# RWKV inverses on packed 32x32 diagonal blocks instead of 64x64 blocks

## The reference: one step of a hybrid trunk

```python
def step(S, inp):                       # per token
    r_t, w_t, k_t, v_t, kk_t, a_t = inp
    sa = jnp.einsum('bhvk,bhk->bhv', S, -kk_t)
    S = (S * w_t[:, :, None, :] + sa[..., None] * (kk_t * a_t)[:, :, None, :]
         + v_t[..., None] * k_t[:, :, None, :])
    return S, jnp.einsum('bhvk,bhk->bhv', S, r_t)
```

## Time and profile before

| | us |
|---|---|
| Median of 3 runs | 1288.97 (1288.81 to 1289.48) |
| The profiled execution: its time | 1288.66 |
| Its span (first to last instruction) | 1286.8 |
| PE busy | 1229.0 (96%) |
| DVE busy | 920.9 (72%) |
| ACT busy | 716.3 (56%) |
| The stage with the inverses, layer 0 | 72 to 165 |
| The same stage, layer 1 | 590 to 685 |

### The profile page before, as it was taken

How to read it: one execution, slowest core, us unless ns; L and a number is a source line. 1 busy time by engine, 2 the same in 40 slices (tenths; PEclk the granted TensorE clock), 3 DMA queues, 4 the chain that set the end, 5 groups by cost and what they waited for, 6 DMA issues and landing times.

```text
span 1286.8 us, 27073 instructions
## 1 busy us (share of the span) xinstructions
PE 1229.0 (96%) x10557; PEld 1098.7 (85%) x10557; DVE 920.9 (72%) x1477; ACT 716.3 (56%) x1109; POOL 131.5 (10%) x161
## 2 busy tenths in 40 slices
PE   7989999899999999998999989899999999999996
PEld 6979888789999999997988878887888788788785
DVE  7576755666555557857675565588989989998996
ACT  6633345234433334472434534577877878777784
POOL 1021310210000000102121012001010110101010
PEclk9999999789999999999999988999999999999998
DMA  8321331155445443242133106389979979997992
GB/s 295 120 85 46 111 106 35 73 198 188 150 152 168 152 147 132 75 134 70 54 119 107 35 23 232 122 292 330 341 256 356 323 263 344 324 354 253 358 323 104
DMA packets 63835, 236.35 MB, mean 184 GB/s; under 512 B 7536, under 2 KB 7760, under 8 KB 63088
## 3 DMA queue, kind: packets, MB, share of 16 engines
q1 hardware_dynamic: 60960, 221.51, 49.1%
q0 software_dynamic: 2336, 12.81, 2.7%
q10 hardware_dynamic: 432, 0.52, 0.1%
HBM read 225.41 MB, written 8.09 MB: 181 GB/s over the span
## 4 chain that ended last, share of the span: by engine, by line
PE 82%; DVE 10%; ACT 4%; issue 4%; DMA 0%; DVEq 0%; ACTq 0%
PE bank L619 12%; PE bank L621 11%; PE bank L620 11%; PE bank L1409 8%; PE bank L1386 6%; PE bank L1388 6%; PE bank L1387 6%; PE bank L613 3%; PE bank L1306 2%; DVE wlo L1981 2%; ACT whi L1472 2%; PE bank L813 1%; PE bank L802 1%; PE bank L809 1%; PE bank L1351 1%
## 5 line engine op out<-in xcount | busy, mean ns | idle before, releaser
L1472 ACT ACTIVATE whi<-wraw 128x1024 fp32r<-128x1024 f32 x407 | 428.8, 1059 | 354.7 <-PE bank L621 292.5
L1981 DVE TENSOR_TENSOR wlo<-wraw,whi 128x1024 fp32r<-128x1024 f32 x407 | 501.4, 1245 | 170.4 <-ACT whi L1472 162.9
L619 PE MATMUL bank<-hh,whi 128*128 128x320 f32 x576 | 189.1, 328 | 12.6 <-DVE Dx L2095 6.4
L621 PE MATMUL bank<-hh,wlo 128*128 128x320 f32 x576 | 180.5, 313 | 0.0
L620 PE MATMUL bank<-hl,whi 128*128 128x320 f32 x576 | 180.5, 313 | 0.0
L1386 PE MATMUL bank<-whi,hh 128*128 128x512 f32 (+1 forms) x384 | 147.4, 384 | 3.4 <-DVE wlo L1981 2.9
L1388 PE MATMUL bank<-wlo,hh 128*128 128x512 f32 (+1 forms) x384 | 143.5, 374 | 0.0
L1387 PE MATMUL bank<-whi,hl 128*128 128x512 f32 (+1 forms) x384 | 143.3, 373 | 0.0
L619 PEld LDWEIGHTS bank<-hh,whi 128*128 128x128 f32 x576 | 110.3, 191 | 23.9 <-issue 7.9
L619 PE MATMUL bank<-rawh,whi 128*128 128x320 f32 x384 | 119.8, 312 | 0.5 <-DVE rawl L2538 0.3
L621 PE MATMUL bank<-rawh,wlo 128*128 128x320 f32 x384 | 118.9, 310 | 0.0
(11 more groups left out here) (427 smaller groups left out, 2084.4 us busy)
## 6 DMA issues: line engine op xcount, KB each, us to landing
wraw<-in_w SPq DMA_DIRECT2D x410, 512.0 KB, 5.0
smb<-in_s_ssm POOLq DMA_DIRECT2D x2, 1536.0 KB, 8.0
out_o_ssm<-smb POOLq DMA_DIRECT2D x2, 1536.0 KB, 7.2
cst<-in_consts SPq DMA_DIRECT2D x1, 2097.0 KB, 13.3
srw<-in_s_rwkv POOLq DMA_DIRECT2D x2, 768.0 KB, 5.9
out_o_rwkv<-srw POOLq DMA_DIRECT2D x2, 768.0 KB, 3.7
x<-in_x SPq DMA_DIRECT2D x2, 640.0 KB, 4.9
cBs<-cB SPq DMA_DIRECT2D x16, 80.0 KB, 2.1
```

What stands on the lines that cost most here:

```text
L619: mm(out, hi, rh, start=first, stop=False)
L621: return mm(out, lo, rh, start=False, stop=last)
L1472: af(whi[:, ring % HI, :], wraw[:, POS[ring], :], ACT.Copy).then_inc(S("slot_hi"), 1)
L1981: tt(wlo[:, POS[ring], :], wraw[:, POS[ring], :], whi[:, ring % HI, :].bitcast(F32), ALU.subtract).then_inc(S("slot_split"), 1)
```

## The change

The inverses of the 32x32 diagonal blocks are held by themselves. A matrix of 64x64 on 64 rows becomes two of 32x32: rows 0 to 31 hold the upper left block, rows 32 to 63 the lower right one (u = 0 and 1), and `Wm`, `TM` and a new `Tq` have 32 columns a place. Levels 1 to 4 run on these. `quads` are the four tiles `o32(o, u)` of 32 rows and 32 columns on the array's diagonal. Level 5 of blocks 0 and 1 becomes two products of the 32x32 blocks around the off-diagonal block of A, which DVE has kept unmasked in columns 32 to 63 of `A`, and the full `TT` is then put together. Block 2 has three levels and stays in `Tq`; L881 reads `Tq` on four tiles there. The number of pieces of each part is as before (12, 12 and 6 on PE; 14, 14 and 8 on DVE), and no TURNS list changes. The constants in HBM are smaller by 96 columns.

```diff
 # PE, inverse(l, b)
-                        for r in map(o64, range(2)):
-                            m = mm(B[A_BANK[b]][r, (c * TA + t) * CH:(c * TA + t + 1) * CH], aa[r, t, cs], X2[r, t, cs],
+                        for u in range(2):
+                            us = slice(cs.start + 32 * u, cs.start + 32 * u + 32)
+                            to = cs if b < 2 and u == 0 else us
+                            at, w = (c * TA + t) * CH, to.stop - to.start
+                            for o in range(2):
+                                m = mm(B[A_BANK[b]][o32(o, u), at:at + w], aa[o64(o), t, us], X2[o64(o), t, to],
...
-                    for r in map(o64, range(2)):
-                        m = mm(B[bk][r, h * CH:(h + 1) * CH], Wm[r, b, h, :], C("i64", rows=r), start=True, stop=True)
+                    for r in quads:
+                        m = mm(B[bk][r, h * 32:(h + 1) * 32], Wm[r, b, h, :], C("i32", rows=r), start=True, stop=True)
-                for q in range(1, LEVELS[b]):
+                for q in range(1, min(LEVELS[b], 5)):
...                   # L802, L809, L813 likewise: for r in quads, 32 and 16 columns
+                if LEVELS[b] == 6:
+                    yield
+                    pe.wait_ge(S(f"inv_dve{b}"), inv_dve(l, b, 11))
+                    for h in heads:
+                        for o in range(2):
+                            m = mm(B[bk][o32(o, 1), h * 32:(h + 1) * 32], A[o32(o, 0), b, h, 32:64], TM[o32(o, 0), b, h, :],
+                    m.then_inc(S(f"inv_pe{b}"), 1)
+                    yield
+                    pe.wait_ge(S(f"inv_dve{b}"), inv_dve(l, b, 12))
+                    for h in heads:
+                        at = n * 32 + h * 32
+                        for u in range(2):
+                            for o in range(2):
+                                lo = o32(o, 1)
+                                m = mm(B[bk][o32(o, u), at:at + 32], C("i32", rows=lo) if u else Wm[lo, b, h, :], Tq[lo, b, h, :],
 # PE, rwkv(l, b): L881
-                        for r in map(o64, range(2)):
-                            m = mm(B[SA_BANK[b]][r, t * HD:(t + 1) * HD], TT[r, b, c * TA + t, :], Rs[r, t, :],
+                        for r in [o32(o, u) for u in range(2) for o in range(2)] if b == 2 else map(o64, range(2)):
+                            m = mm(B[SA_BANK[b]][r, t * HD:(t + 1) * HD], Tq[r, b, t, :] if b == 2 else TT[r, b, c * TA + t, :],
 # DVE, inverse(l, b)
+                if b < 2:
+                    for r in (o32(0, 0), o32(1, 0)):
+                        cp(A[r, b, 0:n, 32:64], b64(A_BANK[b], n, r)[:, :, 32:64])
...                   # all masks, sums and levels on 32 columns a place instead of 64
+                if LEVELS[b] == 6:
+                    yield
+                    v.wait_ge(S(f"inv_pe{b}"), inv_pe(l, b, 11))
+                    cp(Wm_, b32(bk, 0, n)).then_inc(S(f"inv_dve{b}"), 1)
+                    yield
+                    v.wait_ge(S(f"inv_dve{b}"), inv_dve(l, b, 11))
+                    tt(TT[:, b, :, 0:32], Tq_, rep(C("low"), n), ALU.mult)
+                    v.wait_ge(S(f"inv_pe{b}"), inv_pe(l, b, 12))
+                    cp(TT[:, b, :, 32:64], b32(bk, n * 32, n)).then_inc(S(f"inv_dve{b}"), 1)
```

More of the change, by code:

```diff
@@ L429, in trunk @@
         top[0] = raw_at + KEEP * D * 4
-        A, Wm, TM = (sb(n, [P, 3, HA, CH]) for n in ("A", "Wm", "TM"))
+        A = sb("A", [P, 3, HA, CH])
+        Wm, TM = (sb(n, [P, 3, HA, 32]) for n in ("Wm", "TM"))
         brx = sb("brx", [P, TA, T])
@@ L501, in half1, with b32, o32 @@
             return ap.rearrange("p (a o s) -> p a o s", o=2, s=1 << q)[:, :, odd, :]
+        def b32(b, lo, k, rows=slice(0, P)):
+            return B[b][rows, lo:lo + k * 32].rearrange("p (a c) -> p a c", c=32)
+        def o32(o, u):
+            return slice(64 * o + 32 * u, 64 * o + 32 * u + 32)
         def o64(o):
@@ L777, in inverse @@
                 c0, nch, bk = BLOCKS[b][0], CHUNKS_OF[b], INV_BANK[b]
-                heads = range(nch * TA)
+                n = nch * TA
+                heads = range(n)
+                quads = [o32(o, u) for u in range(2) for o in range(2)]
                 yield
@@ L800, in inverse @@
                     for h in heads:
-                        for r in map(o64, range(2)):
-                            m = mm(B[bk][r, h * CH:(h + 1) * CH], A[r, b, h, :], TM[r, b, h, :], start=True, stop=True)
+                        for r in quads:
+                            m = mm(B[bk][r, h * 32:(h + 1) * 32], A[r, b, h, 0:32], TM[r, b, h, :], start=True, stop=True)
                     m.then_inc(S(f"inv_pe{b}"), 1)
@@ L879, in rwkv @@
                     for t in range(TA):
-                        for r in map(o64, range(2)):
-                            m = mm(B[SA_BANK[b]][r, t * HD:(t + 1) * HD], TT[r, b, c * TA + t, :], Rs[r, t, :],
-                                   start=True, stop=True)
+                        for r in [o32(o, u) for u in range(2) for o in range(2)] if b == 2 else map(o64, range(2)):
+                            m = mm(B[SA_BANK[b]][r, t * HD:(t + 1) * HD], Tq[r, b, t, :] if b == 2 else TT[r, b, c * TA + t, :],
+                                   Rs[r, t, :], start=True, stop=True)
                     m.then_inc(S("rw_SA"), 1)
@@ L2233, in inverse @@
                     v.wait_ge(S(f"inv_dve{b}"), inv_dve(l, b, 2 * q + 1))
[L2234 removed]
+                    for mt, odd in ((TM_, 0), (Tq_, 1)):
                         if odd or q < LEVELS[b] - 1:
[L2236 removed]
+                            at = n * 32 + odd * n * 16
+                            got = B[bk][:, at:at + n * 16].rearrange("p (x s) -> p x s", s=1 << q)
                             part = mt.rearrange("p h (a o s) -> p (h a) o s", o=2, s=1 << q)[:, :, odd, :]
```

45 lines of the change are left out of this document (27 added, 18 removed).

## The result

The changed kernel takes 1310.35 us (median of 4 runs, 1307.06 to 1312.32) against 1289.22 us for the kernel before beside it: 1.0161 of its time, 95% interval 1.0136 to 1.0186. The forecast was 1273, faster. It is 21 us slower, and outside the range given.

A forecast was written before the change was run, and what follows sets the result against it. PE was taken to bound the kernel, busy 1229.0 of 1286.8 us, with DVE behind it at a few places. Of its saving 8.2 us a layer arrives, 16.4 in both: from 1288.66 to about 1272.3, taken as 1273; range 1266 to 1286.

The forecast's parts named there:

- A step of 48 passes in 0.38 us: Inverse steps on PE: 24 matmuls on four tiles cost 12 periods of 32 ns, against 0.70 us for 12 matmuls before.
- The floor of 25 ns: Contrary rule: matmul starts never under about 25 ns apart, making the changed kernel cost 33 us more; not applied across tiles.
- PE spared 10.7 us a layer: PE's work in the inverses: 9.6 us less for blocks 0 and 1, 1.1 less for block 2, each layer.
- 82 to 115: ... All arrives: Layer 0, 82 to 115 us: PE never waits, DVE is ahead, so all 5.6 us spared arrives.
- 115 to 127: Layer 0, 115 to 127 us: nine steps spare 2.9 us; with DVE's TM behind a Mamba chain, about 1.2 arrives.
- The first rival: PE's pass starts stay 27 ns apart on any tile: 1329 us; start distance or something else 12%; two tiles only, near nothing, 6%.
- The clock: Rival: half-clock stretches shift, 1269 to 1277 us, or ten us a layer in the inverses: 1283; lost clock or handshake 17%.
- DVE's busy time 6 to 9 us down: Sign to check: shorter DVE operations in the inverses lower its busy time by 6 to 9 us in both layers.
- Waits on DVE up by under 4 us a layer: Sign for the inverses: PE's waits on DVE rising over 4 us a layer would show the handshake forecast wrong.
- The handshake: Rival: shortened PE steps wait for DVE, and DVE for ACT; a layer gains 3 us: 1283 us; with lost clock 17%.
- PE busy in the stage of layer 0 down by 8 us: Sign to check: PE's busy time in layer 0's inverse stage falls by about 8 us.

The follow-up runs named there:

- e1: Kernel before with bursts of small f32 matmuls on constants behind its last work; four 32x32 tiles, N = 32: 8.5 ns a pass, then 128 passes each 3.5 to 3.7 us.
- e5: Kernel before with six artificial PE stalls a layer, no thin tiles or added matmuls: 1321.80 us, 1.0223 of the kernel before.
- e14: Kernel before, its own f32 form, with PE's order of e13 (control): 1298.83 us, 1.0059 of the kernel before.
- e13: Changed kernel in f32, dense half slots cut into quarters and two-product pieces split, spread between steps in place: 1300.37 us, 1.0075 of the kernel before.
- e6: Changed kernel with the inverse's operands in bf16, one pass and two instructions a matmul, same tiles and order: 1283.87 us, 0.9943 of the kernel before.
- e9: Kernel before (two 64x64 tiles) with the inverse's operands in bf16, one pass a matmul: 1276.66 us, 0.9866 of the kernel before.
- e8: Kernel before with bursts on constants mixing four-tile steps and wide matmuls: no stall at 15.0 ns an instruction, four stalls in twelve rounds at 13.4.

## Why the prediction was wrong

- *A step of 48 passes in 0.38 us*: right, 0.42 measured. Tiles do run side by side. The floor of 25 ns of the Trainium skill (TensorE: Matmul & The Clock Gate, section "Wait — 56ns, not 53.3ns?"), weighed there and set aside, is none across tiles: e1 has 32 ns on one tile, 16 on two, 8.5 on four.
- *PE spared 10.7 us a layer*: right as far as the trace can tell, where it is what remains of a sum. Layer 0 has 6.9 us of stalls for instructions, 1.4 more of waits on DVE, and 12.5 + 13.5 us at half clock, of which 45%, 11.7 us, is lost: 20.0 in all. It lost 10.3, so 9.7 were saved. Layer 1: 8.7 of stalls, 1.3 more of waits on DVE, and 35 us more at half clock than before, 15.7: 25.7; it lost 15.2, so 10.5.
- *"82 to 115: ... All arrives"*: this step failed, and "115 to 127" after it. 5.6 us were to be gained there; from the wide matmul at 89.0 us to that at 110.3 the changed kernel lost 3.1 us, and 2.9 more by 124.1. The prediction had gone through data, queues and busy engines, and PE had a wait for none of them. It never counted PE's instructions, though the table that it used gave them (907 passes and as many loads in 48 us are 26 ns for each instruction; in the steps themselves it is 29.2 / 2 = 14.6 ns). The change makes that 18 and, in a step, 4.4 ns. The term missing from the sum: past a store of some 500, no 256 instructions in less than some 3.5 us. In its place the runs showed 6.9 and 8.7 us of stalls for instructions in the two stages, and the half clock that lies behind most of them.
- *The first rival, "the passes don't come faster when there are more of them"*, had the right direction, and by chance the right figure: its 27 ns a pass came from one-column passes on one tile, and e1's sustained 27 to 29 ns has another cause. What it wrote in its own favour holds: no stretch of the trace has four tiles with short passes for long. It was built on the array, though, and priced for all 1656 passes (1329 us). The limit lies ahead of the array and binds only past some 500 instructions in a row, so it cost less, and something else with it.
- *The clock*: named, and mis-sized. I allowed ten us in each layer at half; it is 26 and 38, and it costs more than the stalls themselves: 27 us of the two layers' loss against 15.6. It was expected from thinner matmuls; e1 and e5 show that they don't lower the clock and that a pause of PE can. One part is not the change's: a half-clock stretch at 71 us lies behind a wait that both kernels have (3.1 us at 68.6), and e14, in the old form, has a clock of 0.97 there too.
- *DVE's busy time 6 to 9 us down*: 920.9 to 914.3, right; the copies on 32 rows took 348 ns each (0.35 taken). *Waits on DVE up by under 4 us a layer*: right, 1.4 and 1.3. But the waits cost more than their length: two stretches at half clock in layer 0 lie behind them, some 3 us, and more of what is left in e13. The handshake took a part after all, by way of the clock, which its rival had not priced.
- *PE busy in the stage of layer 0 down by 8 us*: it is, 90.7 to 82.6 in the earlier trace rows's two stretches, and proves nothing: the stretches hold less of the work.

The Trainium skill (Runtime: NRT & Kernel Launch, section "Instruction fetch mechanics") has the mechanism: each engine's instructions come in blocks of 16 KiB, 256 instructions, the next fetched while one is worked off. The packets of 16 KB, the 251 passes ahead of the first stall and the 256 instructions between stalls agree. It also says that crossing a block's border is "mostly hidden". For thin matmuls the runs say otherwise: in e1's burst with N = 32 each border behind the store costs 1.5 to 2.7 us. This page bore on the change from the start, and the prediction did not draw on it.

Open: what makes one pause of PE lower the clock and another not (1.47 us in e5, 1.49 in e1 and 2.2 in e6 didn't, 1.81 in e6 and 1.2 in e13 were followed by half clock), and why a finer order costs the old form 8 us.

## What to carry to other kernels

Count an engine's instructions beside its busy time: here TensorE got at best some 256 each 3.5 us, and a change that makes matmuls shorter and more numerous must leave any 256 in a row that much work, or PE runs dry once its store is used up. Halving the instructions was worth more than doubling the tiles (e9 against e6, in bf16). And where TensorE at a full clock gets pauses of one to three microseconds, count them more than once: 18.5 us of them cost 31.5 in e5. A new order needs its control on the old code.

## What the runs showed of the hardware

- Four 32x32 tiles, f32, N = 32: starts 8.5 ns apart as long as instructions last; N = 64: 259 passes in 3.87 us, 14 ns, and then a stall of 1.49 us; two tiles 16 ns, one tile 32 ns.
- Sustained, PE took 128 f32 passes each 3.5 to 3.7 us in e1, after a store of 251 (259 with N = 64); in the changed kernel borders in a row were 3.5 to 4.7 us apart.
- 4.2 ns an instruction in a burst against 13.6 to 14.6 sustained: a factor of three that the steps of the kernel before could not show, since they asked for one each 14 to 15 ns.
- Instruction stalls stood whole multiples of 256 instructions apart, in the changed kernel, e1 and e8, and ended 2.2 to 3.0 us after the start of a packet of the instruction queue.
